# Scan stage of a two-block mixer kernel: first loads ahead of the first gate store, four reload slots, an earlier mask, 14 gate products moved forward

## The chip, the cores and the metric

One core of one Trainium2 chip. The metric is the device time of one execution in microseconds (us). TensorE is called PE here, its weight load PEld, VectorE DVE, ScalarE ACT, GpSimd POOL, and SyncE, which issues the DMAs, SP.

## The reference, cut to what matters

The program computes two blocks. The second one, `hybrid_layer`, projects the normalised input to all its streams, runs four mixers, and adds them with gates:

```python
h = rmsnorm(x, norm_gain)
proj = h @ w_in
(gdn_qkv, gdn_a, gdn_b, gdn_z, sg_u, sg_v, sg_z, rw, rw_z,
 nsa_q, nsa_kv, nsa_g, nsa_z, merge) = jnp.split(proj, IN_OFFSETS, axis=-1)
ys = (gated_deltanet(...), spatial_gating(...), rwkv7_time_mix(...), native_sparse_attention(...))
gates = jnp.split(jax.nn.sigmoid(merge), N_MIXERS, axis=-1)
mixed = gates[0] * (ys[0] @ w_branch[0])
for i in range(1, N_MIXERS):
    mixed = mixed + gates[i] * (ys[i] @ w_branch[i])
return x + mixed @ w_out
```

`merge` is 4096 columns wide (32 tiles of 128) for 1024 positions. It doesn't depend on the mixers, so its product can be done at any time before the end. Spatial gating multiplies by weights that are masked to be causal.

## The kernel before, in words

Activations lie transposed, 128 features on the partitions and 1024 positions in the free dimension. Each float32 product is made of three float32r matmuls (high by high, high by low, low by high), so every operand is kept as a high part and the remainder. Weights come as one stream of chunks of eight 128x128 blocks: SP loads a chunk into one of three raw slots (L294), ACT rounds it to its high part (L304), POOL subtracts for the low part (L312), and PE waits for the low part. The two split chunks are reused as soon as PE has used the chunk two before.

The stages that matter here are these.

**Projections** (`hybrid_in_*`). For each of 30 tiles PE makes 24 matmuls (L359), DVE scales the result into one of four stage buffers (L2558), ACT applies a function (L2606) where the tile has one, and SP stores it to HBM (L2640). Entries 22 to 27 of the list are plain copies, the last two go through Silu. After the last tile DVE multiplies the spatial gating weights by a triangular mask (L2586, 128x512), and then every engine passes a fence ("hy projected"): PE waits for the last instruction of DVE, ACT and POOL. SP waits for these and for the last four stores as well.

**Scans** (`scans_*`). Every engine runs the same order, written as Python generators. `weave_beside` takes turns between two streams: stream 0 is the gated delta net (gdn) and then the first part of the sparse attention (nsa), stream 1 is spatial gating (sg) and then rwkv. Each turn is a weave step. After each step comes one step of a third generator, the gates, and at the steps listed in `MORE_GATES` come more of them. A gate step on PE is one product of the `merge` projection: three 128x512 matmuls at L454. There are 512 of them, two halves of the positions (q) by 32 tiles (m) by 8 input blocks (i). Counting from 0, product 256 q + 8 m + i is the i-th of tile m. Two gate steps after a tile's last product come, on their engines, its scaling in PSUM (DVE L2681), its sigmoid (ACT L2698), its store to HBM (SP L2721), and on SP the load of a further weight chunk. Each engine executes its instructions in this order, so an engine that waits holds back everything behind the waiting instruction.

**The second half of the gates.** The first half (q = 0) uses the split left by the entry, for positions 0 to 511. For q = 1 the same buffers are filled again: in gate steps 250 to 257, one block i each, SP loads x from HBM into a slot of `XB` (L2716), ACT makes the high part (L2703) once product 248 + i has used the old one, DVE the low part (L2685), and product 256 + i waits for that. There are two slots. The loads of blocks 0 and 1 go out with the store of tile 29 (gate step 241); that of block i + 2 waits on SP for the low part of block i.

**Where the order puts them.** There are 381 weave steps on PE, and `MORE_GATES` adds 70, so 451 products lie among the scans. Before weave step s the number of products done is s - 1 plus the extras of the steps below s: 13 before step 2, 250 at the last of step 213, 255 at the last of step 215. SP has 374 steps and takes the same extras.

**Start of the scans on SP.** After the fence SP issues three loads for gdn and its `zy` (L2766), then the 13 gate steps of weave step 1, which hold the store of gate tile 0 (gate step 9) and so wait for it, and then in steps 2 and 4 the six loads of spatial gating, three for each j. PE's first instruction of step 2 is the spatial mean (L2847), which waits for the three of j = 0.

**Attention** (`attend_streams`). 24 gate steps lead, then eight attention streams are woven with the gate steps that are left, one after each step: 512 - 451 - 24 = 37 products, at attention steps 1 to 37 of 233. Attention itself is PE L3999, L4005 and L4011, DVE L4028 to L4042, ACT L4056 and L4062. Then follow the branch products, the output product and the last norm.

Of the kernel before, what the change touches and what calls it, by code (L numbers as in the profile page):

```python
# [835 lines left out]
def wait_steps(n):  # L836
    for _ in range(n):
        yield
# [1598 lines left out]
def mixer1_sync(sy, K, M, chunk0):  # L2437
# [8 lines left out]
               *[("copy", 0)] * 6, *[("silu", 0)] * 2]  # L2446
NP = len(PROJECTIONS)
NM = 32
FUNCTIONS = {"silu": ACT.Silu, "gelu": ACT.Gelu_apprx_tanh, "copy": ACT.Copy, "sigmoid": ACT.Sigmoid}

# [94 lines left out]
def hybrid_in_vector(ve, K, H):  # L2545
    V = K.V
# [16 lines left out]
    def evac(g):  # L2563
# [12 lines left out]
        elif kind == "shift":  # L2576
            ve.own().tensor_tensor(st, pd[:, 2:2 + T], pd[:, 3:], SUB).then_inc(*V())
            ve.own().scalar_tensor_tensor(out=st, in0=st, scalar=K.vec("rw_mu", arg), in1=pd[:, 3:], op0=MUL, op1=ADD).then_inc(*V(("staged", g)))
        elif kind == "copy":
            scaled_into(st, "hp", g, slice(0, 128), ("staged", g))  # L2580
        else:
            scaled_into(st, "hp", g, slice(0, 128), ("plain", g))

    project2_drive(chain((0,), walk(ve, K, nothing, 8, NP, first=1)), evac, small_rows_vector(ve, K, H))
    ve.wait_ge(*K.at("hybrid constants"))
    ve.own().tensor_tensor(H.sg_w[:, :, :], H.sg_w[:, :, :], K.upper.unsqueeze(1).to_broadcast([128, 4, 128]), MUL).then_inc(*V(("causal sg",)))  # L2586
    ve.fence(K, "hy projected")
# [87 lines left out]
def gates_vector(ve, K, N, R):  # L2675
# [7 lines left out]
    def between(i):  # L2683
        ve.wait_ge(*K.at("second high", i))
        ve.own().scalar_tensor_tensor(out=H[:, 1, i, :], in0=R.XB[:, i % 2, :], scalar=N.gain(i), in1=H[:, 0, i, :].bitcast(F32), op0=MUL, op1=SUB).then_inc(*K.V(("second low", i)))  # L2685

# [3 lines left out]
def gates_scalar(se, K, N, R):  # L2690
# [9 lines left out]
    def between(i):  # L2700
        se.wait_ge(*K.at("second x", i))
        se.wait_ge(*K.at("used", i))
        se.own().activation(H[:, 0, i, :], R.XB[:, i % 2, :], ACT.Copy, scale=N.gain(i)).then_inc(*K.S(("second high", i)))  # L2703

# [7 lines left out]
def gates_sync(sy, K, N, R, chunk0):  # L2712
    def second(i):
        if i >= 2:
            sy.wait_ge(*K.at("second low", i - 2))
        sy.e.dma_start(R.XB[:, i % 2, :], K.keep[:, i, HIGH]).then_inc(*K.x_in[i % 2](("second x", i)))  # L2716

    def evac(q, m):
# [4 lines left out]
        if (q, m) == (0, NM - 3):  # L2723
            second(0)
            second(1)

    def between(i):
        if i + 2 < 8:
            second(i + 2)

# [1414 lines left out]
class Scans:  # L4145
    def __init__(self, K, H):
# [3 lines left out]
        self.gates = K.sb([128, 2, 512], ctx=self.late_scope, name="gates")  # L4150
        self.XB = K.sb([128, 2, 512], ctx=self.late_scope, name="xb")
        self.right_scope = Scope("right")
# [16 lines left out]

MORE_GATES = {1: 12, 18: 3, 51: 2, 59: 5, 96: 2, 133: 4, 139: 5, 176: 2, 213: 3, 215: 3, 252: 6, 256: 8, 297: 7, 351: 2, 361: 6}  # L4170

# [40 lines left out]
def in_turn(*streams):  # L4212
    for s in streams:
        yield from s
# [53 lines left out]
def scans_sync(sy, K, R, chunk0):  # L4268
    g, s, w, B = R.gdn, R.sg, R.rw, R.nsa

    def rwkv_first():
        yield from wait_steps(12)
        for j in range(2):
# [6 lines left out]
    weave_beside(gates, in_turn(gdn_sync(sy, K, g, lambda: nsa_load(sy, K, B)), nsa_sync(sy, K, B)),  # L4280
                 in_turn(rounds(spatials(lambda j: spatial_sync(sy, K, s, j)), rwkv_first()), wait_steps(RWKV_LATER), rwkv_sync(sy, K, w)), more=MORE_GATES)

# [674 lines left out]
def program(nc, A, at):  # L4957
    with Scope() as ctx:
# [19 lines left out]
        K.xs, K.w_raw, K.stage_out = ([K.dma(f"{n}{i}") for i in range(k)] for n, k in (("x", 4), ("w", NRAW), ("stage", NSTAGE)))  # L4978
        K.x_in, K.gate_out = ([K.dma(f"{n}{i}") for i in range(2)] for n in ("xh", "go"))
        K.back, K.gate_back = [K.dma(f"y{i}") for i in range(2)], [K.dma(f"g{i}") for i in range(3)]  # L4980
# [40 lines left out]
```

## Time and profile before

| | |
|---|---|
| time, median of 3 runs | 4180.58 us (4179.37 to 4186.12) |
| the profiled execution's own time | 4175.23 us |
| its span, first to last instruction | 4173.4 us |
| mean granted TensorE clock | 0.964 |
| PE busy | 3898.7 us (93%) |
| DVE busy | 2679.8 us (64%) |
| ACT busy | 1449.4 us (35%) |
| POOL busy | 1202.5 us (29%) |
| chain that ended last | PE 71%, DVE 21%, ACT 4% |

All times inside the program count from the start of the span. The scans run from about 2875 to 3750 us, the attention from there to 3958 us. Busy shares are over the span; a wait of PE inside a stage with PE in its chain is what a change can win back. A granted clock of 1.00 is the higher level of PE's clock, 2.4 GHz, and 0.50 the lower one, 1.2 GHz.

### The profile page before, as it was taken

The page shows a single profiled execution, that of the slowest core. Times are in us where ns is not written, and L with a number is a line of the kernel's source. Part 1 is how long each engine was busy: PE and PEld are TensorE (multiplying, and loading weights), DVE is VectorE, ACT ScalarE, POOL GpSimd, SP SyncE. Part 2 cuts the span into 40 slices and gives each one's busy share as a digit, 9 for nine tenths or more (in the row PEclk, how much of TensorE's full clock was granted, in tenths as well). Part 3 has the DMA queues.
Part 4 walks back from the last instruction along what each step waited for, and adds up shares of the span by engine and source line. Part 5 has one row for each costly group of instructions (what it writes and reads, how often), then busy time and mean ns, then how long its engine had stood idle before and what let it go on. Part 6 is the DMA issues. An engine that isn't in the chain of part 4 may idle for free.

```text
span 4173.4 us, 47439 instructions
## 1 busy us (share of the span) xinstructions
PE 3898.7 (93%) x18382; PEld 3094.4 (74%) x18382; DVE 2679.8 (64%) x3001; ACT 1449.4 (35%) x1896; POOL 1202.5 (29%) x583
## 2 busy tenths in 40 slices
PE   8999899999879999989999988998999989998988
PEld 6557788877656666778887867886788878876777
DVE  6764787889764554378778988531655555546783
ACT  4334432234333333243223433212333333325512
POOL 2002134445413333213444531222222112212054
PEclk9999999999989999999999999998999989999999
DMA  3002223345320000222334532223211221323054
GB/s 110 20 16 81 101 91 104 96 153 189 115 76 21 21 26 21 86 101 87 113 104 158 172 119 105 98 101 113 83 62 54 71 76 61 110 73 106 22 206 141
DMA packets 130874, 382.36 MB, mean 92 GB/s; under 512 B 13460, under 2 KB 14104, under 8 KB 125400
## 3 DMA queue, kind: packets, MB, share of 16 engines
q1 hardware_dynamic: 130648, 379.32, 27.4%
q8 instruction: 145, 2.38, 0.2%
q14 instruction: 81, 0.66, 0.1%
HBM read 278.08 MB, written 101.19 MB: 91 GB/s over the span
## 4 chain that ended last, share of the span: by engine, by line
PE 71%; DVE 21%; ACT 4%; issue 1%; DMA 1%; POOL 1%; SPq 0%; DVEq 0%; ACTq 0%; POOLq 0%
PE ps L359 22%; PE ps L1389 20%; PE ps L454 7%; PE ps L872 3%; PE ps L2875 2%; PE ps L2881 2%; PE ps L4342 2%; PE ps L2182 1%; DVE acc L1658 1%; PE ps L2174 1%; DVE top L1562 1%; DVE xop L1562 1%; PE ps L2936 1%; DVE x L636 1%; PE ps L2862 1%
## 5 line engine op out<-in xcount | busy, mean ns | idle before, releaser
L312 POOL TENSOR_TENSOR wlo<-wraw,whi 128x1024 fp32r<-128x1024 f32 x185 | 455.7, 2463 | 1764.8 <-ACT whi L304 1630.9
L1389 PE MATMUL ps<-xop,whi 128*128 128x512 f32 x1984 | 616.7, 392 | 15.5 <-DVE acc L1683 10.1
L304 ACT ACTIVATE whi<-wraw 128x1024 fp32r<-128x1024 f32 x185 | 196.0, 1060 | 907.6 <-PE ps L359 626.4
L1389 PE MATMUL ps<-top,whi 128*128 128x512 f32 x1488 | 470.0, 397 | 22.3 <-DVE acc L1652 17.0
L1389 PEld LDWEIGHTS ps<-xop,whi 128*128 128x128 f32 x1984 | 372.2, 188 | 100.2 <-DVE acc L1683 12.6
L1389 PE MATMUL ps<-xop,wlo 128*128 128x512 f32 x992 | 387.7, 391 | 0.0
L454 PE MATMUL ps<-xhalf,whi 128*128 128x512 f32 x1024 | 363.6, 437 | 4.8 <-ACT n L4056 3.5
L1389 PEld LDWEIGHTS ps<-top,whi 128*128 128x128 f32 x1488 | 281.5, 190 | 91.1 <-DVE acc L1652 20.3
L359 PE MATMUL ps<-xhi,whi 128*128 128x512 f32 x900 | 322.9, 441 | 23.2 <-DVE xlo L656 6.7
L1784 POOL TENSOR_TENSOR wlo<-wsum,whi 128x1024 fp32r<-128x1024 f32 (+2 forms) x102 | 229.4, 2249 | 368.0 <-ACT whi L1414 367.4
L1389 PE MATMUL ps<-top,wlo 128*128 128x512 f32 x744 | 294.5, 396 | 0.0
L359 PE MATMUL ps<-xlo,whi 128*128 128x512 f32 x900 | 286.6, 400 | 0.0
L359 PE MATMUL ps<-xhalf,whi 128*128 128x512 f32 x1012 | 274.9, 394 | 11.2 <-DVE xhalf L656 8.8
L359 PE MATMUL ps<-xhi,wlo 128*128 128x512 f32 x900 | 284.2, 397 | 0.0
L1784 POOL TENSOR_TENSOR wlo<-wraw,whi 128x1024 fp32r<-128x1024 f32 (+2 forms) x80 | 180.1, 2251 | 244.3 <-ACT whi L1414 242.5
L359 PEld LDWEIGHTS ps<-xhi,whi 128*128 128x128 f32 x900 | 169.2, 196 | 86.5 <-issue 34.3
L359 PEld LDWEIGHTS ps<-xhalf,whi 128*128 128x128 f32 x1012 | 191.6, 190 | 53.7 <-DVE xhalf L656 10.7
L1389 PEld LDWEIGHTS ps<-xop,wlo 128*128 128x128 f32 x992 | 186.5, 188 | 41.1
L454 PEld LDWEIGHTS ps<-xhalf,whi 128*128 128x128 f32 x1024 | 173.5, 196 | 46.9 <-issue 21.6
L1414 ACT ACTIVATE whi<-wsum 128x1024 fp32r<-128x1024 f32 (+2 forms) x108 | 101.8, 943 | 304.0 <-PE ps L1389 126.4
L454 PE MATMUL ps<-xhalf,wlo 128*128 128x512 f32 x512 | 205.7, 402 | 0.0
L359 PEld LDWEIGHTS ps<-xlo,whi 128*128 128x128 f32 x900 | 175.2, 195 | 39.1
(625 smaller groups left out, 7424.7 us busy)
## 6 DMA issues: line engine op xcount, KB each, us to landing
wraw<-in_w_dram SPq DMA_DIRECT2D x185, 512.0 KB, 3.7
h_keep<-h SPq DMA_DIRECT2D x154, 256.0 KB, 4.8
wraw<-in_s_dram SPq DMA_DIRECT2D x48, 512.0 KB, 4.2
f<-h_keep SPq DMA_DIRECT2D x24, 768.0 KB, 5.7
wmore<-in_s_dram SPq DMA_DIRECT2D x32, 512.0 KB, 4.2
x_keep<-x SPq DMA_DIRECT2D x16, 1024.0 KB, 3.9
g_keep<-gates SPq DMA_DIRECT2D x64, 256.0 KB, 2.4
gb<-g_keep SPq DMA_DIRECT2D x32, 512.0 KB, 3.6
```

Source lines behind the costliest of these rows:

```text
L304: se.own().activation(K.hi(c), K.raw[:, c % NRAW, :], ACT.Copy).then_inc(*K.S(("hi", c)))
L312: ge.own().tensor_tensor(K.lo(c), K.raw[:, c % NRAW, :], K.hi(c).bitcast(F32), SUB).then_inc(*K.G(("lo", c)))
L359: done = pe.e.matmul(into[:, h, :], wt, x[h], start=(first and j == 0), stop=(last and j == 2), skip_group_check=True)
L454: done = mm(K.ps[:, b, :], wt, x, start=(i == 0 and j == 0), stop=(i == n - 1 and j == 2), skip_group_check=True)
L872: d = mm(K.ps[:, banks[h], :], M.diag[:, (BY_PE.index(j) * TAPS + k) % NDIAG, :], M.Yc[:, j, 512 * h + k:512 * h + k + 512], start=(k == 0 ...
L1389: d = pe.e.matmul(out[:, s, :], w[:, o], x[:, i, :], start=(j < 3 and i == 0 and t == 0), stop=(i == k - 1 and t == 2), skip_group_check=True)
L1414: se.own().activation(F.whi(c), F.source(b, j), ACT.Copy).then_inc(*K.S((n, "whi", c)))
L1562: ve.own().tensor_tensor(F.olo[j][:, :k, :], source[:, :k, :], F.ohi[j][:, :k, :].bitcast(F32), SUB).then_inc(*K.V((F.name, "op", g, j)))
L1784: seat.own().tensor_tensor(F.wlo(c), F.source(b, j), F.whi(c).bitcast(F32), SUB).then_inc(*signal((F.name, "wlo", c)))
L2875: d = mm(K.ps[:, b, part(i)], I.AT[:, part(i)], I.T[:, part(i)], start=True, stop=True, skip_group_check=True)
L2881: d = mm(K.ps[:, b, part(i)], I.X[:, part(i)], I.TT[:, part(i)], start=True, stop=True, skip_group_check=True)
L4342: done = mm(into, w, x, start=(i == 0 and j == 0), stop=(i == 7 and j == 2), skip_group_check=True)
```

## The change

The mask on the spatial gating weights goes from the end of the projections to just after the first plain copy (entry 22). `XB` gets four slots and four semaphores, so the loads of blocks 0 to 3 go out together and that of block i + 4 waits for the low part of block i. `MORE_GATES` gets 14 more products, at or before nine steps. On SP a list of its own, `LOADS_AHEAD`, gives the extras of step 1 at step 4.

```diff
+COPIES = [g for g, (kind, _) in enumerate(PROJECTIONS) if kind == "copy"]
+NXB = 4
 ...
         elif kind == "copy":
             scaled_into(st, "hp", g, slice(0, 128), ("staged", g))
+            if g == COPIES[0]:
+                ve.wait_ge(*K.at("hybrid constants"))
+                ve.own().tensor_tensor(H.sg_w[:, :, :], H.sg_w[:, :, :], K.upper.unsqueeze(1).to_broadcast([128, 4, 128]), MUL).then_inc(*V(("causal sg",)))
 ...
     project2_drive(chain((0,), walk(ve, K, nothing, 8, NP, first=1)), evac, small_rows_vector(ve, K, H))
-    ve.wait_ge(*K.at("hybrid constants"))
-    ve.own().tensor_tensor(H.sg_w[:, :, :], H.sg_w[:, :, :], K.upper.unsqueeze(1).to_broadcast([128, 4, 128]), MUL).then_inc(*V(("causal sg",)))
     ve.fence(K, "hy projected")
 ...
     def second(i):
-        if i >= 2:
-            sy.wait_ge(*K.at("second low", i - 2))
-        sy.e.dma_start(R.XB[:, i % 2, :], K.keep[:, i, HIGH]).then_inc(*K.x_in[i % 2](("second x", i)))
+        if i >= NXB:
+            sy.wait_ge(*K.at("second low", i - NXB))
+        sy.e.dma_start(R.XB[:, i % NXB, :], K.keep[:, i, HIGH]).then_inc(*K.x_in[i % NXB](("second x", i)))
 ...
         if (q, m) == (0, NM - 3):
-            second(0)
-            second(1)
+            for i in range(NXB):
+                second(i)
 
     def between(i):
-        if i + 2 < 8:
-            second(i + 2)
+        if i + NXB < 8:
+            second(i + NXB)
 ...
-        self.XB = K.sb([128, 2, 512], ctx=self.late_scope, name="xb")
+        self.XB = K.sb([128, NXB, 512], ctx=self.late_scope, name="xb")
 ...
-MORE_GATES = {1: 12, 18: 3, 51: 2, 59: 5, 96: 2, 133: 4, 139: 5, 176: 2, 213: 3, 215: 3, 252: 6, 256: 8, 297: 7, 351: 2, 361: 6}
+MORE_GATES = {1: 15, 7: 2, 18: 3, 51: 2, 59: 5, 86: 2, 92: 3, 96: 2, 133: 5, 139: 5, 176: 3, 213: 3, 215: 4, 217: 1, 252: 6, 256: 8, 297: 7, 351: 2, 361: 6}
+LOADS_AHEAD = {**MORE_GATES, 1: 0, 4: 15}
 ...
-                 in_turn(rounds(spatials(lambda j: spatial_sync(sy, K, s, j)), rwkv_first()), wait_steps(RWKV_LATER), rwkv_sync(sy, K, w)), more=MORE_GATES)
+                 in_turn(rounds(spatials(lambda j: spatial_sync(sy, K, s, j)), rwkv_first()), wait_steps(RWKV_LATER), rwkv_sync(sy, K, w)), more=LOADS_AHEAD)
 ...
-        K.x_in, K.gate_out = ([K.dma(f"{n}{i}") for i in range(2)] for n in ("xh", "go"))
+        K.x_in, K.gate_out = ([K.dma(f"{n}{i}") for i in range(k)] for n, k in (("xh", NXB), ("go", 2)))
```

With the 14 more, 465 products lie among the scans and 23 in the attention. Before weave step 213 twelve more are done than before, so products 248 to 255 come at weave steps 202 to 209 and gate steps 250 to 257 at steps 204 to 211, one after each step, where they were at steps 213 to 217.

## Rows read from the trace of the kernel before

**Rows 1.** The page: shares of the chain that ended last, by engine.

```profile
PE 71%; DVE 21%; ACT 4%; issue 1%; DMA 1%; POOL 1%; SPq 0%; DVEq 0%; ACTq 0%; POOLq 0%
```

**Rows 2.** Waits between 2870 and 3766: who for whom, total, times, longest.

```profile
PE ps L2936 <- DVE r L3549: 15.2, 3, 12.2
```

**Rows 3.** Timeline of the scans' start: start, duration, instruction, [idle before it].

```profile
2871.87 2.36 POOL L312 TENSOR_TENSOR wlo<-wraw,whi 128x1024 fp32r<-128x1024 f32 x1 [8.45 <-ACT whi L304]
...
2872.07 2.70 DVE L2586 TENSOR_TENSOR sgw<-sgw,const 128x512 f32<-128x512 f32 x1
...
2874.88 2.08 PE L2847 MATMUL ps<-rows,c 4*128 4x512 f32 x4 [4.23 <-DVE sgw L2586]
...
2876.88 1.22 PE L454 MATMUL ps<-xhalf,whi 128*128 128x512 f32 x2
...
2877.09 0.43 SPq L2766 DMA_DIRECT2D zy<-p_keep  x1
...
2886.10 0.62 PE L454 MATMUL ps<-xhalf,whi 128*128 128x512 f32 x2
...
2886.78 0.62 PE L454 MATMUL ps<-xhalf,whi 128*128 128x512 f32 x2
...
2888.21 3.23 SPq L2766 DMA_DIRECT2D sg<-p_keep  x6
...
2897.08 3.78 PE L2847 MATMUL ps<-sg,c 128*128 128x512 f32 x4 [9.45 <-DMA sg<-p_keep]
...
2901.41 1.84 PE L2781 MATMUL ps<-c,g 128*128 128x2 f32 x16
...
2910.82 3.42 PE L2781 MATMUL ps<-c,sg 128*128 128x2 f32 x16 [1.83 <-ACT sg L2821]
```

**Rows 4.** Stretches at the lower clock: length, PE busy (matmuls), granted clock, DMA.

```profile
2890.55:2900.79 10.24, 3.71 (x5) 0.50 0.80 322
2911.03:2917.86 6.83, 6.83 (x29) 0.50 0.39 115
...
3382.07:3399.14 17.07, 5.79 (x23) 0.50 0.38 123
3402.55:3409.38 6.83, 5.06 (x18) 0.50 0.37 115
...
sum 78.51, PE 57.53; mean PE 4.79
```

**Rows 5.** Timeline around the reload: SP's loads, POOL, PE's waits.

```profile
3375.98 14.18 SPq L2716 DMA_DIRECT2D xb<-x_keep  x6
...
3386.87 2.39 POOL L312 TENSOR_TENSOR wlo<-wraw,whi 128x1024 fp32r<-128x1024 f32 x1 [12.03 <-ACT whi L304]
...
3393.35 2.07 PE L2936 MATMUL ps<-r 64*128 64x128 f32 x8 [12.24 <-DVE r L3549]
...
3404.32 2.08 PE L2936 MATMUL ps<-r 64*128 64x128 f32 x8 [3.75 <-DVE inv L3504]
```

**Rows 6.** High and low parts of the reload: minimum, median, maximum ns, first and last start.

```profile
L2703 ACT ACTIVATE xhalf<-xb,vec x8: 721/722/725, 3374.4 to 3402.0; 128x512 fp32r<-128x512 f32 x8
L2685 DVE SCALAR_TENSOR_TENSOR xhalf<-xb,vec,xhalf x8: 750/751/2169, 3375.2 to 3402.8; 128x512 fp32r<-128x512 f32 x8
```

**Rows 7.** Windows: length, busy PE, PEld, DVE, ACT, POOL, clock, DMA, GB/s.

```profile
3354.50:3368.50 14.00, 14.00 (x103) 12.77 (x102) 10.22 (x21) 9.79 (x15) 6.18 (x3) 1.00 0.23 69
3354.50:3410.40 55.90, 39.90 (x230) 34.62 (x230) 39.11 (x60) 23.18 (x32) 10.99 (x5) 0.79 0.31 99
3795.00:3811.00 16.00, 16.00 (x85) 13.30 (x84) 11.50 (x35) 13.59 (x25) 4.84 (x2) 1.00 0.41 125
3811.00:3958.00 147.00, 129.76 (x790) 98.61 (x788) 113.16 (x381) 89.59 (x217) 7.64 (x4) 0.98 0.04 14
```

**Rows 8.** Two of four smaller waits of PE among the scans: timeline.

```profile
3103.95 1.13 PE L2936 MATMUL ps<-g 64*128 64x128 f32 x8 [2.75 <-DVE g L3089]
...
3197.45 1.84 PE L2936 MATMUL ps<-r 64*128 64x128 f32 x8 [2.62 <-DVE r L3549]
```

More of the change, by code:

```diff
@@ L2684, in between @@
         ve.wait_ge(*K.at("second high", i))
-        ve.own().scalar_tensor_tensor(out=H[:, 1, i, :], in0=R.XB[:, i % 2, :], scalar=N.gain(i), in1=H[:, 0, i, :].bitcast(F32), op0=MUL, op1=SUB).then_inc(*K.V(("second low", i)))
+        ve.own().scalar_tensor_tensor(out=H[:, 1, i, :], in0=R.XB[:, i % NXB, :], scalar=N.gain(i), in1=H[:, 0, i, :].bitcast(F32), op0=MUL, op1=SUB).then_inc(*K.V(("second low", i)))
     yield from gate_tiles(lambda: walk(ve, K, nothing, 8, NM), evac, between)
@@ L2702, in between @@
         se.wait_ge(*K.at("used", i))
-        se.own().activation(H[:, 0, i, :], R.XB[:, i % 2, :], ACT.Copy, scale=N.gain(i)).then_inc(*K.S(("second high", i)))
+        se.own().activation(H[:, 0, i, :], R.XB[:, i % NXB, :], ACT.Copy, scale=N.gain(i)).then_inc(*K.S(("second high", i)))
     yield from gate_tiles(lambda: walk(se, K, weights_scalar, 8, NM), evac, between)
```

## The prediction

> **What bounds the kernel now.** I read the page's chain first: PE holds 71% of it [rows 1], so time is lost where PE waits or runs at its lower clock. The list of waits then names who made it wait among the scans; its longest wait of PE is 12.2 us, for DVE L3549 [rows 2]. The timeline around each long wait gives the places. There are two large ones. At the start PE stands still for 9.45 us until the spatial gating loads land at 2897.08; SP issued them only at 2888.21, behind the store of gate tile 0 [rows 3]. At the reload for the second half PE stands still for 12.24 us and then for 3.75 us [rows 5]. SP spends 14.18 us on its last six loads, because each waits for a slot of two, and DVE, which must make the low parts in order, reaches L3549 late. Four more waits of 2.0 to 2.8 us lie between; two are in [rows 8]. After most of these PE runs at a granted clock of 0.50: the twelve stretches at 0.50 from 2873 to 3461 contain 57.53 us of busy PE [rows 4]. In the attention's gate steps the reader is to see PE full, 16.00 of 16.00 us, and after the last product at 3811 not full, 129.76 of 147 [rows 7].
>
> **The change, part by part.**
>
> *The mask.* It takes 2.70 us of DVE, 2872.07 to 2874.77, and PE starts 0.11 us later, at 2874.88 [rows 3]. Without it the fence still waits for POOL's last low part, 2871.87 + 2.36 = 2874.23. PE then starts at 2874.34: gain 0.54 us, not 2.7. In its new place the 2.70 us lie beside PE's products of the next tile, with DVE idle between tiles; if that cover were gone it would cost 2.7.
>
> *First loads ahead.* SP's loads for gdn and `zy` end at 2877.52 [rows 3] and stay, since they wait for the last projection store. Now only one gate step follows before the loads of sg j = 0, so they go out from about 2877.6 instead of 2888.21. The three landed 2897.08 - 2888.21 = 8.9 us after the first issue. The same delay gives 2886.5; if they also queue behind gdn and `zy`, at most some 3 us more, 2889.5. PE meanwhile has 16 products instead of 13. The 13 took 2876.88 to about 2887.6, 10.75 us; a further one takes 2886.78 - 2886.10 = 0.68 us [rows 3]. So PE reaches the spatial mean at 2876.34 + 10.75 + 2.04 = 2889.1. Against 2897.08 that is 7.9 us, the mask's 0.54 in it; I take 7.6 for the loads' spread. What is late next is neither DMA nor the gate store (tile 0 is ready at about 2887.4, and SP's six loads are out by 2881), but ACT: its split of the chunk behind product 15 now stands at the end of step 1. It has nothing urgent behind it.
>
> *The clock there.* With no idle stretch at 2888 to 2897 the stretch 2890.55 to 2900.79 need not be at 0.50; its 3.71 us of busy PE would take 1.86 [rows 4]. The wait of 1.83 us at 2910.82 [rows 3] gets two products (1.36), and what follows it, 6.83 us busy at 0.50 [rows 4], could give 3.4. The waits behind are chains over POOL and DVE, which don't shrink with the clock. I take 1.8 for the first and nothing to 5.3 for the rest, value 1. Start in all: 7.6 + 1.8 + 1 = 10.4 us, bounds 6 and 15.
>
> *Four slots.* By the weave's count the eight pairs of high and low part come at steps 204 to 211 instead of 213 to 217, one per step. Loads of blocks 0 to 3 go out nine steps ahead, the others four steps ahead of use, with 2 to 3 us per step; the DMA waits vanish. The pairs cost the same work: 8 x 0.75 on DVE, 8 x 0.72 on ACT [rows 6]. Queued behind each low part is all that DVE does for both streams, and PE waits for that. The new place is the window 3354.5 to 3368.5, where PE is full, DVE busy 10.22 and ACT 9.79 of 14 us [rows 7]. With the pairs added they have 16.2 and 15.6 us for 14, so this window stretches by at least 2.2 us. In exchange the wait at L3549 shrinks. For the whole passage, 3354.5 to 3410.4, the floors are: PE 39.90 busy, of which 5.79 + 5.06 at 0.50 [rows 4], so 39.9 - 5.4 + two products more, 35.9 us; DVE 39.11 busy less 1.4 for its one long low part, plus some 0.03 between 60 instructions, 39.5 us. The passage can't fall below 39.5 of 55.9, a gain of 16.4. From the other side, if each pair stalls DVE by one more microsecond and the waits for DVE of 2.62 us remain as in the earlier unit at 3197.45 [rows 8], it is 39.5 + 8 + 2.6 = 50.1, a gain of 5.8. I take 44.5, nearer to the floor, because two steps lie between product 248 + i and its pair: gain 11.4 us.
>
> One long low part stands in [rows 6]: 2169 ns against a median of 751, begun while POOL's L312 of 3386.87 ran [rows 5]. The Trainium skill, "GPSIMD Engine Reference", section "Specifications", says that POOL shares its way into SBUF with DVE and that DVE instructions with two SBUF inputs contend with it. A low part has two. By that rule POOL's 6.18 us of the new window [rows 7] would hit three or so of the eight low parts, at 1.4 us each, and the passage would be 48.7 instead of 44.5; by the trace's other seven low parts, hardly any.
>
> *Fourteen more products.* Three are counted above. Eleven go before waits: two before the 1.83, two before a wait of 2.4, three before 2.75, one each before 2.62 and 2.0, two in the reload passage. There they fill idle time and don't move the end of a wait. If the gap is gone or elsewhere they cost 0.68 each; the seven at the four middle places could lose 4.8. On the other side, shorter idle stretches may keep the clock up: the stretches behind these four places hold about 20 us of busy PE in the sum of [rows 4], 10 us to win. I take 2, near the low end, since the waits shrink and stay.
>
> *The end.* The products leave the attention's steps 24 to 37. There PE is full, 16.00 us for 14 products and the attention's share [rows 7], so 14 x 0.68 = 9.5 us leave the bound. The next bound is DVE, 11.50 busy in that window, 1.4 of it gate scaling, and its density afterwards is 113.16 / 147 = 77% [rows 7]: 10.1 / 0.77 = 13.1, a gain of 2.9. ACT loses its gate work as well (13.59 busy falls most). The 24 leading products stay 24, and attention's first loads go out as before. Bounds 2.9 and 9.5; I take 7, because the whole stretch from 3776 has less PE and ACT work, not only this window.
>
> *Sum.* 10.4 + 11.4 + 2 + 7 = 30.8 us. The profiled execution took 4175.23 us (span 4173.4 and 1.8 around it), 5.35 under the median of the runs, 4180.58. So 4144.4 for it, and 4149.8, say 4150, as a median.
>
> **The rivals.**
> 1. *The reload's stall only moves.* DVE and ACT are over-full in steps 204 to 211, and in order, so PE waits there instead. For it: 16.2 us of DVE work for 14. Against: DVE and ACT have 17 and 33 us free in the whole passage. The passage gains 5.8, the middle -2 and the end 2.9: 10.4 + 5.8 - 2 + 2.9 = 17, time 4163.
> 2. *The clock stays up.* The twelve stretches hold 57.53 us of busy PE, 29 to win. For it: waits of 9.45 and 12.24 us stand just before the two longest. Against: stretches follow waits of 2.0 us too. With the start at 15, the passage at 16, the middle at 6 and the end at 9: 46, time 4135. The Trainium skill, "TensorE: Matmul & The Clock Gate", section "Part 1: The HAM clock gate", has it that the throttled state is the default and activity lifts it; by that rule products in place of waits pay twice, as here. The trace agrees as to the order of events [rows 4].
> 3. *Slower.* The low part waits for the high part of the same gate step, and the high part for product 248 + i; where DVE, ACT and PE take turns on these waits, the eight steps become a chain, and everything of both streams waits in it. It costs eight times the price of a turn. The stalls that it replaces are 12.24 + 3.75 = 16 us and the other parts give 19.4, so it decides the sign from 35.4 / 8 = 4.4 us a step. With 6 us a step: 48 - 35.4 = 13 slower, 4193. Against: PE needs low part i only six products later.
> 4. *The loads don't come earlier*, because the change's order on SP meets a wait that I don't see. Then only three filled products and the fence remain at the start, 1 us instead of 10.4: 4159.
>
> **How the numbers follow.** Forecast 0.60, rival 1 0.18, rival 2 0.12, rival 4 0.06, rival 3 0.04. The forecast's own terms reach 22 to 40 us of gain, 4141 to 4159. With rival 1 whole and most of rival 2, the range is 4136 to 4168. The measurement tells changes of 0.2%, 8.4 us, from none. Faster than that: forecast, rivals 2 and 4, and 0.14 of rival 1: 0.92. Within 0.2%: 0.05. Slower: 0.03.
>
> **What would show it.** PE's mean L2847 starts near 2889 with no wait for DMA above 1 us. PE's first L2847 waits for POOL's L312 rather than for DVE. SP's eight loads of `xb` don't spread over 24 us but the first four go out in 2 us, and ACT L2703 waits for no DMA. The wait for L3549 falls from 12.2 to under 4 us, and the window of the eight pairs is 2 to 5 us longer. The last L454 product comes some 30 us before 3811. It would be wrong if the passage takes over 50 us, or if attention from its first product to its end keeps its length.

## The result and the profile after

| | median us | range | runs |
|---|---|---|---|
| before | 4177.85 | 4167.89 to 4186.47 | 20 |
| after | 4187.49 | 4179.94 to 4193.81 | 20 |

The ratio is 1.0022, 95% interval 1.0015 to 1.0029: the change makes the kernel 9.6 us slower, where 4150 was forecast, with 0.03 for slower.

The profiled execution of the changed kernel took 4185.32 us, its span is 4183.5, PE is busy for 3909.2 us (before 3898.7) at a mean clock of 0.965, DVE 2684.5, ACT 1452.8, POOL 1208.0. From line 2587 of the kernel before up to its list `MORE_GATES` a line's number is 3 higher in the changed kernel (L2681 is L2684, L2698 is L2701, L2847 is L2850, L2936 is L2939, L3549 is L3552). The page's chain, which answers to [rows 1]:

```profile
PE 69%; DVE 23%; ACT 4%; issue 1%; POOL 1%; DMA 1%; DVEq 0%; SPq 0%; ACTq 0%; POOLq 0%
```

The waits of PE between 2870 and 3766, which answer to [rows 2] (total us, times, longest):

```profile
PE ps L2865 <- ACT g L2841: 9.3, 3, 4.4
PE ps L2939 <- DVE r L3552: 5.0, 3, 2.4
PE ps L2850 <- DVE r L3542: 4.0, 2, 3.2
PE ps L2850 <- POOL wlo L312: 3.8, 1, 3.8
```

The wait of 12.2 us is gone. At the top stands a new one: PE waits for L2841, a copy out of PSUM on ACT.

The start, timeline (as [rows 3]):

```profile
2878.40 1.13 PE L2850 MATMUL ps<-rows,c 4*128 4x512 f32 x4 [3.84 <-POOL wlo L312]
...
2881.47 3.24 SPq L2769 DMA_DIRECT2D sg<-p_keep  x6
...
2892.09 1.88 PE L2850 MATMUL ps<-sg,c 128*128 128x512 f32 x4
```

The loads go out before any gate store, the mean waits for nothing and begins 13.7 us after PE's first scan instruction; before it was 2897.08 - 2874.88 = 22.2 us [rows 3].

The reload, timeline and the durations of low and high parts (as [rows 5, 6]):

```profile
3347.49 1.89 SPq L2719 DMA_DIRECT2D xb<-x_keep  x4
...
3366.26 6.15 SPq L2719 DMA_DIRECT2D xb<-x_keep  x4
...
3387.30 1.10 PE L2850 MATMUL ps<-r,c 128*128 128x512 f32 x2 [3.20 <-DVE r L3542]
```

```profile
L2706 ACT ACTIVATE xhalf<-xb,vec x8: 723/726/727, 3363.8 to 3382.1; 128x512 fp32r<-128x512 f32 x8
L2688 DVE SCALAR_TENSOR_TENSOR xhalf<-xb,vec,xhalf x8: 750/752/1721, 3365.5 to 3382.9; 128x512 fp32r<-128x512 f32 x8
```

The passage and the attention behind its last product, windows (as [rows 7]); in a window of 56 us around the reload PE now gets through 322 matmuls and is busy for 50.5 us, where it was 230 and 39.9 of 55.9:

```profile
3358.00:3414.00 56.00, 50.54 (x322) 42.83 (x320) 42.74 (x67) 30.51 (x43) 13.42 (x6) 0.97 0.30 95
3814.00:3962.00 148.00, 128.65 (x755) 95.82 (x755) 115.17 (x394) 88.88 (x221) 7.06 (x3) 0.98 0.04 13
```

Lastly the whole stretch from PE's first scan instruction to the first matmul of the projection behind the attention, with PE alone (window, length, busy PE, its matmuls, clock, DMA), and behind it the sum over those parts of it in which the granted clock is 0.50. First the kernel before:

```profile
2874.90:3959.00 1084.10, 1009.90 (x6243) 0.96 0.23 73
...
sum 97.59, PE 76.21; mean PE 4.76
```

The changed kernel:

```profile
2878.40:3969.20 1090.80, 1020.84 (x6243) 0.95 0.23 73
...
sum 98.96, PE 92.80; mean PE 5.46
```

The reader is to see three numbers. Idle PE: 74.2 us before, 70.0 after, so the products did fill idle time. Busy PE at the lower clock: 76.2 before, 92.8 after. Matmuls take about twice as long there (a pair of L454 1.22 us at 0.50 and 0.62 at 1.00 [rows 3]), so half of the 16.6 more is lost, 8.3 us. The rest, busy time less half of the low part, is 971.8 and 974.4. Together -4.2 + 8.3 + 2.6 = +6.7 us, the growth of the stretch; the other 3.5 of the span lie ahead of it. There the profiles differ by more than that from one execution to the next: PE's first scan instruction starts at 2878.4 in this one and at 2868.5 in that of e8 below, whose projections are the same. So from here on I compare times that count from this instruction.

To see where, I compare the start of each PE instruction in both traces, relative to the first scan instruction. Minus is earlier than before:

| at (time before) | after against before | what lies in between |
|---|---|---|
| 2923 | -14.4 us | start without the wait for loads |
| 2962 | -2.3 | new waits of 1.80 and 4.38 us, and 17 us at the lower clock |
| 3350 | +4.2 | small waits, some filled, some new |
| 3418 | -7.2 | reload: 11.4 us won |
| 3527 | +1.6 | new wait of 3.54 us and 13.7 us at the lower clock |
| 3663 | +10 | |
| 3766 | +15.8 | |
| 3958 | +6.8 | attention, with 14 products fewer, 9.0 us won |

Start, reload and end give what was forecast for them or more. Between them 12.1 + 6.5 + 8.8 + 14.2 = 41.6 us are lost, at places where the forecast had a gain of 2. The products themselves are the small part of it. Five of the fourteen lie in the start and two in the reload; the other seven all lie between 2962 and 3350, 7 x 0.68 = 4.8 us if each costs its full price. The remaining 12.1 + 8.8 + 14.2 = 35.1 us are lost in stretches to which no product was added.

**The loss at 2937 to 2955.** Timeline of the changed kernel:

```profile
2932.49 2.45 POOL L312 TENSOR_TENSOR wlo<-wraw,whi 128x1024 fp32r<-128x1024 f32 x1 [9.04 <-ACT whi L304]
2933.49 2.00 DVE L2894 TENSOR_TENSOR inv<-inv,c 128x512 f32<-128x512 f32 x1
...
2936.37 0.63 PE L2865 MATMUL ps<-const,inv 128*128 128x128 f32 x4 [1.80 <-DVE inv L2895]
...
2937.97 1.22 DVE L3333 TENSOR_TENSOR sg<-sg 128x1024 f32<-128x1024 f32 x1
2939.30 0.70 DVE L2684 TENSOR_TENSOR ps<-ps,t 128x512 f32<-128x512 f32 x1
2940.03 0.60 ACT L2701 ACTIVATE gates<-ps 128x512 f32<-128x512 f32 x1 [6.35 <-DVE ps L2684]
...
2940.72 1.29 ACT L2841 ACTIVATE g<-ps 128x512 f32<-128x512 f32 x2
...
2941.37 1.11 PE L2865 MATMUL ps<-const,inv 128*128 128x128 f32 x4 [4.38 <-ACT g L2841]
```

Read it from the end. PE waits for ACT's copy L2841. It is short and its input is there, but ACT is in order, and in front of it stands the sigmoid of a gate tile, L2701. That waits 6.35 us for the tile's scaling L2684 on DVE, and the scaling stands in turn behind spatial gating's and gdn's vector work. So work that PE needs now queues behind work that nobody needs yet. The clock falls 1 us into that wait, at 2937.9, and stays down for 13.6 us behind its end, in which PE is full:

```profile
2937.90:2954.97 17.07, 13.60 (x48) 0.50 0.43 139
```

At 3505 the same chain recurs, again with L2684, L2701, L2841 in a row:

```profile
3502.61 2.43 POOL L312 TENSOR_TENSOR wlo<-wraw,whi 128x1024 fp32r<-128x1024 f32 x1 [6.82 <-ACT whi L304]
3502.79 2.81 DVE L2895 TENSOR_TENSOR inv<-const,inv 128x512 f32<-128x512 f32 x1
...
3507.21 0.70 DVE L2684 TENSOR_TENSOR ps<-ps,t 128x512 f32<-128x512 f32 x1
3507.94 0.60 ACT L2701 ACTIVATE gates<-ps 128x512 f32<-128x512 f32 x1 [5.41 <-DVE ps L2684]
...
3509.23 1.12 PE L2865 MATMUL ps<-const,inv 128*128 128x128 f32 x4 [3.54 <-ACT g L2841]
```

In both places a DVE instruction of gdn's inverse runs beside POOL's split of a chunk and takes 2.00 and 2.81 us where the one next to it takes 0.69. The Trainium skill ("GPSIMD Engine Reference", section "Specifications") has it that POOL contends with DVE instructions that read two SBUF inputs; these do, and the trace agrees. The delay is handed on: DVE is not idle between L2894 and the tile's scaling, so the 1.3 us extra of the first place are part of PE's waits there, and the 2.1 us extra of the second are part of the 3.54.

Both the tile work and the splits hang on the number of products done: a tile is 8 products and its scaling, sigmoid, store and next load come two gate steps behind the eighth. In the kernel before they stand at places where they harm little. The added products shift them: by 3 from step 1 on, by 5 from step 7, 7 from 86, 10 from 92, then 11, 12, 13 and 14. So two theories were put against each other. **Phase**: what costs is the shift of all later tiles against the streams, and a shift by a multiple of 8 costs nothing. **Rivals**: the three scheduling edits are at fault, the products cost their own time, or the count alone matters. In the expectations below theory A is the phase; B has it that the streams' own chains give back what is won; C that a product costs only where it was added.

### The profile page after: what moved, and what is told of

It is laid out like the page before. It is cut to its first block, busy times and chain, and to the rows that moved or that the text cites. A ratio compares the mean times of both kernels' runs of the same rounds, so it can differ in the third digit from the quotient of the medians.

```text
span 4183.5 us, 47429 instructions
## 1 busy us (share of the span) xinstructions
PE 3909.2 (93%) x18382; PEld 3097.0 (74%) x18382; DVE 2684.5 (64%) x3001; ACT 1452.8 (35%) x1896; POOL 1208.0 (29%) x583
## 4 chain that ended last, share of the span: by engine, by line
PE 69%; DVE 23%; ACT 4%; issue 1%; POOL 1%; DMA 1%; DVEq 0%; SPq 0%; ACTq 0%; POOLq 0%
PE ps L359 21%; PE ps L1389 19%; PE ps L454 7%; PE ps L872 3%; PE ps L2878 2%; PE ps L2884 2%; PE ps L4346 2%; PE ps L2182 1%; DVE top L1562 1%; DVE acc L1658 1%; DVE xop L1562 1%; PE ps L2174 1%; PE ps L2939 1%; DVE t L618 1%; DVE x L636 1%
## 5 line engine op out<-in xcount | busy, mean ns | idle before, releaser
L454 PE MATMUL ps<-xhalf,whi 128*128 128x512 f32 x1024 | 363.2, 437 | 8.8 <-POOL wlo L312 5.4
L454 PEld LDWEIGHTS ps<-xhalf,whi 128*128 128x128 f32 x1024 | 174.2, 197 | 51.6 <-issue 24.0
L454 PE MATMUL ps<-xhalf,wlo 128*128 128x512 f32 x512 | 207.8, 406 | 0.0
```

The costliest lines, as they stand in the source:

```text
L454: done = mm(K.ps[:, b, :], wt, x, start=(i == 0 and j == 0), stop=(i == n - 1 and j == 2), skip_group_check=True)
```

## The experiments

The edits below are against the changed kernel or the one named. Each was timed in five rounds beside the kernel before (4177, 4176 for the last two).

| run | median us | range | ratio to before, 95% |
|---|---|---|---|
| e1 three edits, old products | 4162.45 | 4155.1 to 4165.6 | 0.9968 [0.9956, 0.9980] |
| e2 new products only | 4198.95 | 4191.7 to 4208.0 | 1.0059 [1.0047, 1.0071] |
| e3 loads ahead only | 4163.26 | 4155.7 to 4165.0 | 0.9971 [0.9960, 0.9983] |
| e4 four slots only | 4175.88 | 4166.2 to 4182.8 | 0.9994 [0.9984, 1.0004] |
| e5 e1 + 3 products at step 1 | 4185.75 | 4177.1 to 4194.7 | 1.0019 [1.0008, 1.0030] |
| e6 e1 + 8 | 4162.19 | 4160.1 to 4171.7 | 0.9965 [0.9953, 0.9978] |
| e7 e1 + 3, 3 fewer at step 18 | 4165.52 | 4163.6 to 4166.6 | 0.9970 [0.9961, 0.9980] |
| e8 after, tile work 5 steps later | 4186.67 | 4179.0 to 4194.2 | 1.0023 [1.0013, 1.0032] |
| e9b e1 with six slots | 4163.82 | 4161.1 to 4170.3 | 0.9963 [0.9951, 0.9975] |
| e10b e1 + 4 | 4176.96 | 4163.7 to 4187.7 | 0.9997 [0.9987, 1.0007] |
| e11b e1, middle products moved | 4159.22 | 4155.1 to 4167.4 | 0.9952 [0.9940, 0.9963] |
| e12b e5, tile work 3 steps later | 4173.59 | 4167.8 to 4186.8 | 0.9989 [0.9980, 0.9999] |
| f1 e6 and e11b together | 4163.32 | 4150.7 to 4168.0 | 0.9966 [0.9954, 0.9977] |
| f2 after, 8 more products in place of 14 | 4167.49 | 4163.5 to 4171.9 | 0.9979 [0.9970, 0.9988] |

**Which part of the change.** e1 keeps mask, loads and slots and puts the old products back:

```diff
-MORE_GATES = {1: 15, 7: 2, 18: 3, 51: 2, 59: 5, 86: 2, 92: 3, 96: 2, 133: 5, 139: 5, 176: 3, 213: 3, 215: 4, 217: 1, 252: 6, ...}
+MORE_GATES = {1: 12, 18: 3, 51: 2, 59: 5, 96: 2, 133: 4, 139: 5, 176: 2, 213: 3, 215: 3, 252: 6, ...}
```

> Mask, first loads ahead and four slots together, with the 70 extra gate products where they were. Theory A (the 14 added products change which weave step each gate tile is finished at, and the new meeting points cost more than the rest wins): 15 to 25 us faster than before, with the start and the reload each 8 us or more earlier and nothing given back in between. Theory B (the scans are paced by the chains of the streams over DVE, ACT and POOL, which give back what the start and the reload win): within 5 us of before. The time from the first inverse products at 2953 to 3375 is the same as before within 3 us under A, 8 or more longer under B.

e2 is the kernel before with the new list, on SP too.

> Only the 14 more products, on SP as well; mask, loads and slots as before. Theory A: 15 to 30 us slower than before, with new waits of PE of 3 us or more that end on ACT or DVE work for a gate tile, and lower-clock stretches in which PE is full behind them. Theory B: within 5 us of before, since the products fill waits (minus) and the chains keep their pace.

e1 is 0.32% faster than before, 14 us between the medians, and e2 0.59% slower, 22 us between the medians for 14 products; together 1.0027, near the 1.0022 of the whole change. The edits add up, and the products alone make it slower. e1 stays just short of the 15 us of theory A, and nothing is given back from 2953 to 3375 (12.2 us ahead of the kernel before at both ends), which is against B. e2 shows more than the time. It has none of the three scheduling edits, and yet the new waits of the changed kernel stand in it again, to a few hundredths: 1.79 and 4.37 us for 1.80 and 4.38, then 3.19 for 3.20 and 3.54 for 3.54.

```profile
2952.81 1.12 PE L2862 MATMUL ps<-const,inv 128*128 128x128 f32 x4 [4.37 <-ACT g L2838]
```

e3 and e4 part e1 further: e3 has only `LOADS_AHEAD = {**MORE_GATES, 1: 0, 4: 12}` beside the kernel before, e4 only `NXB = 4`.

> Only the first loads ahead of the first gate store (12 extras of step 1 at step 4 on SP). Theory A: 7 to 11 us faster; PE's wait of 9.45 us before the spatial mean falls to under 2 us and the lead is kept to the end. Theory B: the lead is there at 2930 and gone by 2960; within 3 us of before.

> Only the four slots. The high and low parts stay at weave steps 213 to 217. Theory A: the waits for the DMA (8.4 us on ACT) go, PE's wait at L3549 falls from 12.2 to about 5 us, 6 to 10 us faster. Theory B: the same wait falls but the next chain gives it back, within 3 us of before.

The loads alone give 13 of e1's 14 us, more than the 7 to 11 expected: the lead is 12.8 us at 2937 and still 12.3 at 3958. The slots give nothing in the time that can be told from none. In e4's trace PE's wait falls from 12.2 to 9.2 us, not to 5, and the passage from 3350 to 3418 wins 2.6 us; in e1 it wins 4.0, in e3, without slots, 0.9. So the slots are worth some 3 us there. The mask had no run of its own; e3 and e4 leave nothing of e1 for it. Why four slots help so little without the products is in DVE's order in e1:

```profile
3358.61 1.87 SPq L2719 DMA_DIRECT2D xb<-x_keep  x4
3369.20 9.58 SPq L2719 DMA_DIRECT2D xb<-x_keep  x4
...
3374.63 5.52 DVE L2688 SCALAR_TENSOR_TENSOR xhalf<-xb,vec,xhalf 128x512 fp32r<-128x512 f32 x4
3380.18 0.69 DVE L3614 TENSOR_TENSOR r<-r 128x512 f32<-128x512 f32 x1
...
3382.94 0.69 DVE L3552 TENSOR_TENSOR r<-ps,r 128x512 f32<-128x512 f32 x1
...
3383.68 2.07 PE L2939 MATMUL ps<-r 64*128 64x128 f32 x8 [9.36 <-DVE r L3552]
```

With the old products four low parts stand in one block in front of L3552; one of them, beside POOL's split, takes 2.95 us. In the changed kernel the pairs are spread over weave steps 204 to 211, one step each, the last low part starts at 3382.9, and the longest wait for L3552 is 2.4 us. The gain of the reload belongs to the products that moved the pairs, and hardly to the slots: e2, with two slots, wins nearly all of it, going from 15.3 us behind the kernel before at 3350 to 5.0 at 3418. Six slots in place of four (`NXB = 6`) put the question to the transfers once more:

> The kernel e1 (the three scheduling edits, without the added products) with six reload slots in place of four. In e1 the rwkv step at L3552 behind the reload still waits 9.4 us, the transfers of blocks 4 to 7 being issued only as slots come free. DMA reading (the transfer is what is late): with six slots two more blocks are under way early, that wait falls to about 6 us, and the time is 4157 to 4160. In-order reading (VectorE and ScalarE stand in line, the transfer is only reported as last): the wait falls by less than 2 us and the time stays at 4160 to 4164.

The wait falls from 9.36 to 8.31 us and the time stays (4163.82): the in-order reading holds. ACT waits for no load of `xb` at all now, where it was 6.3 us in e1. Even the 1.05 us aren't the transfers': the block of four low parts takes 4.46 us for 5.52, because its longest one, beside POOL's split, takes 1.90 for 2.95.

```profile
3378.73 2.08 PE L2939 MATMUL ps<-r 64*128 64x128 f32 x8 [8.31 <-DVE r L3552]
```

**Phase or count.** To e1, products at the first place only: `1: 15` (e5), `1: 20` (e6), `1: 15, 18: 0` (e7), `1: 16` (e10b), with the number in `LOADS_AHEAD` alike.

> The three edits, and only the first of the added groups: 3 more products in weave step 1 (15 for 12), so that every later product is one of a tile three products ahead of where it was. Theory A (what counts is the phase of tiles and chunks against the weave steps): the lead of the three edits at 2930 is kept or grows by the lower-clock stretch there, and then falls by 5 to 20 us at places where no product was added; in all 3 to 15 us slower than the three edits alone (they took 4162). Theory C (each added product costs only where it was added): the same time as the three edits within 4 us, since three products cost 2 us at the start and give 2 us back at the end.

> The three edits and 8 more products in weave step 1 (20 for 12), a whole tile and chunk, so that phases are as before from step 2 on. Theory A: no new waits between 2900 and 3370; the 5.4 us that the eight products take at the start come back at the end, and the reload falls into other weave steps, where it may win up to 10 us; 4150 to 4162. Theory C: 4158 to 4166. If the number of products done ahead counted rather than their phase, it would be slower than e5.

> The three edits, 3 more products in weave step 1 and 3 fewer at step 18, so that the phases are as before from step 18 on and differ only from step 1 to 18. Theory A: nothing is lost after about 2935 in comparison with before; 4158 to 4168. Theory C: the same. If it loses as e5 does, the loss comes from the first 18 steps and not from the phase later.

> The three scheduling edits, and four more gate products at the first place (16 where e1 has 12, e5 has 15, e6 has 20): every later gate tile's scaling, sigmoid and store, and every chunk's split, move by half a tile. Phase reading (what counts is at which step of the streams a tile's work falls): any time from 4167 to 4190, the time not lying on the line between e1, e5 and e6. Rival, a smooth effect of the number of products: 3 cost 23 us, 8 cost nothing, so 4 lie on the falling side, at about 4181. Rival, e5's three are an unlucky single collision: 4160 to 4165.

Three more cost 23 us, beyond the 3 to 15 that theory A gave; four cost 15, eight nothing. Three more that are taken back at step 18 cost 3, which the intervals don't tell from none. In the traces, relative to e1, PE's instructions in e7 stand at +3.2 us at 3022 and between +1.6 and +3.8 from there to the end, while those of e5 drift to +36.5 (its profiled execution, 4194.69, was its slowest). e6 stands between +3.0 and +6.5 up to 3347, about the 8 x 0.68 = 5.4 us of its own products, and at +6.7 from 3436 to 3726. So the loss of e5 isn't the number of products, nor their own 0.68 us: it is where later tiles and splits fall. That four cost less than three, and eight nothing, a line through the count can't give. The smooth rival's 4181 for four lies just outside the interval, 4171.8 to 4180.2, and the single collision's 4160 to 4165 well outside; the phase's own range of 4167 to 4190 was so wide that it proves little by itself. Whether the cost within a period of 8 is smooth or the sum of several collisions stays open.

A rival within the phase is that the shift only makes more DVE instructions run beside POOL's splits. It doesn't: what all DVE instructions of the scans took beyond the usual time of their line and shape sums, by my estimate from the traces, to 31 us before, 35 in the changed kernel and 30 in e5. What changes is which of them are hit and who waits behind.

e5 shows in full what the lower clock takes. PE waits 1.93 us at 3715.31 for DVE, and then 1.42 us at 3721.30 for a bank that the sigmoid of a gate tile frees late. No further wait above 0.9 us follows before this stretch, with PE full throughout, of which 10 us are lost:

```profile
3735.90:3756.38 20.48, 20.48 (x72) 0.50 0.15 45
```

**Tile work or splits.** e12b is e5 with the tile work three gate steps later, at about its steps in e1, while products and splits stay three early. With a tile's scaling and sigmoid its store and the load of a further chunk move too. e8 does it to the changed kernel, five steps later (`[None] * 6`).

```diff
-                late += [None, (q, m)]
+                late += [None] * 4 + [(q, m)]
```

> The kernel e5 (three scheduling edits, three more products at the first place, 4185.75 us) with a gate tile's scaling, sigmoid and store queued three gate steps later, so that they stand again at about the steps that they have in e1; the chunks' splits and the products themselves stay three early. If the place of a tile's scaling and sigmoid in the orders of VectorE and ScalarE is the cause of e5's 23 us: 4160 to 4170. If it is the splits or the products themselves: 4180 to 4190. Between these, both have a part.

> The changed kernel with one edit: a tile's scaling, sigmoid and store come seven gate steps after its last product instead of two. Products stay where they are, and so do the splits of the chunks. Theory A with the tile's work as the cause: at 2937 the products are five ahead of before, so the tile's work is back at its old weave steps; the wait of 4.4 us for ACT at 2937 and those near 3010 go, and 8 to 15 us are won by 3050; later, where products are 11 to 14 ahead, it wins or loses. Theory A with the chunks' splits as the cause: the waits near 2937 and 3010 stay.

e12b wins back 12 of the 23 us between e5 and e1, between the two ranges: the place of the tile work has about half of it, the splits and the products themselves the rest; I didn't part these two. e8's time is that of the changed kernel, but its course isn't. In it the waits of 1.80 and 4.38 us near 2937 are gone, as the explanation has it, with one of 2.68 in their place, and it is 9.5 us ahead of the changed kernel at 3043, within the 8 to 15 expected, and 15.6 at 3683. From 3707 on it loses all of this, since PE waits before products instead, 4.64, 2.55, 2.94 and 7.41 us, the last for a chunk:

```profile
3777.16 0.70 DVE L2684 TENSOR_TENSOR ps<-ps,t 128x512 f32<-128x512 f32 x1
3777.30 1.06 ACT L304 ACTIVATE whi<-wraw 128x1024 fp32r<-128x1024 f32 x1 [12.07 <-DMA wraw<-in_w_dram]
...
3781.09 1.19 PE L454 MATMUL ps<-xhalf,whi 128*128 128x512 f32 x2 [7.41 <-POOL wlo L312]
```

SP issues the load of a further chunk behind a tile's store. A later store is a later load, and the chunk's split then holds up PE. So the delay isn't free in itself.

**Does it hold for the change as it is?** f2 is the changed kernel with its products up to step 96, then brought back to 8 more:

```diff
-133: 5, 139: 5, 176: 3, 213: 3, 215: 4, 217: 1,
+133: 2, 139: 5, 176: 2, 213: 3, 215: 3,
```

> The changed kernel (4187.49 us) with eight more products than before in place of fourteen: all of its added ones up to step 96, but 2 at step 133 in place of 5, 2 at 176, 3 at 215 and none at 217, so that behind step 139 every tile is back at the step that it had before. The changed kernel lies 12 us behind e1 at that place and 25 at the end. Phase reading: what it loses behind the place goes, what it loses ahead of it stays, 4170 to 4178. Rival (the loss is that of the products themselves, 22 us for 14, evenly): six fewer give back 9 us, 4178 to 4181. Rival (the order behind is no better with the old places once the start has moved): 4184 to 4190.

It takes 4167.49, ratio 0.9979. From the changed kernel's 1.0022 to e1's 0.9968 are 0.54%, 23 us; six products fewer give back 0.43% of it, 18 us, where they themselves are 6 x 0.68 = 4. That is more than either reading had in its range, and twice what the even loss by count has. In the traces, relative to e1, f2 stands at +12.4 us from 3200 to 3345 and at most 3.5 further back from 3430 to 3800, where the changed kernel goes from +9.1 to +32.6. The sum over its lower-clock parts, where the changed kernel has 92.80:

```profile
sum 83.62, PE 73.76; mean PE 5.27
```

Its 17 us stretch at 2936 is still there, ahead of the place where the phase is restored.

**A faster version.** e11b moves products of the middle earlier and leaves their sum as it was: `86: 2, 92: 3, 133: 1` for `96: 2, 133: 4`. f1 has eight more at step 1 beside that.

> The three scheduling edits, and the middle products moved earlier by a few steps with their number unchanged (2 at step 86 and 3 at 92 in place of the 2 at 96 and 3 of the 4 at 133): the waits of 2.4 and 2.8 us of the kernel before at these steps are filled, and behind step 133 every tile keeps its place. Phase reading: between steps 86 and 133 tiles move by 2 to 5 products, which costs or gains a few us, and nothing moves behind: 4157 to 4168, with the waits of 2.4 and 2.8 us under 1.5. Reading by the count alone (a filled wait is won, nothing else matters): 4158 or less.

> The three scheduling edits, eight more gate products at the first place (20 where e1 has 12), and the middle products moved earlier as in e11b. Phase reading: eight keep every tile at its place, so the two changes add up: e6's 4162 and e11b's 4159 give 4156 to 4163. Count reading (products cost about 0.68 us each wherever they fall, and 8 are far from nothing): 4164 to 4170.

e11b is the fastest that I ran, 0.48% under the kernel before; its interval overlaps with e1's, so that the moved products add something isn't shown. In its trace the waits of 2.41 and 2.75 us are 1.03 and 1.84, the second not under 1.5 as expected, and the later one of 2.62 has grown to 4.09. f1 is no better than either, between the ranges of phase and count: it doesn't tell the two apart.

## Why the prediction was wrong

*The mask*, 0.54 us: PE's first wait fell from 4.23 [rows 3] to 3.84, 0.39 us, and is for POOL, as forecast. Right.

*First loads ahead and the clock there*, 10.4: 14.4 us by the traces of the whole change, with the five products that were put in there, and 13 by e3's median without any. Right, at the upper bound. The spatial mean came 8.5 us earlier, for about 7.4 by the forecast's own places; the rest, 5.9, is what followed it, where 2.8 were taken. The stretch at 0.50 at 2890 [rows 4] went with the wait.

*Four slots*, 11.4: the passage did win 11.4 us (+4.2 to -7.2) and the wait for L3552 is 2.4 us, under the 4 that were given as the mark. The size was right, to the tenth by luck with bounds of 5.8 and 16.4, and the owner wrong. I counted the pairs' new weave steps and the slots as one edit; e4, e1 and e9b show that the slots alone win some 3 us there, since DVE's block of low parts, not the transfer, was last, and e2 that the products alone win 10.3. Of the eight low parts one ran beside POOL's split, 1.72 us for 0.75, not three.

*The end*, 7: 9.0 us, right within its bounds.

*Fourteen more products*, 2 us won: this step failed. "There they fill idle time and don't move the end of a wait. If the gap is gone or elsewhere they cost 0.68 each" priced a product by itself, on PE alone. The gaps did fill: 2.41, 2.75, 2.62 us became 1.38, 1.06, 2.39, and PE is idle for 4.2 us less in all. But each product also moves every later tile's scaling, sigmoid, store and load, and every chunk's split, in the orders of DVE, ACT, SP and POOL. I had that shift in hand and used it only where it helped, at the reload ("by the weave's count the eight pairs ... come at steps 204 to 211"). What is theirs in the forecast (the reload's 11.4, the middle's 2, the end's 7) is a gain of 20.4; e2 measured a loss of 22.3, 42.7 us off. The remaining 10.4 were measured as 14.2 in e1. 14.2 - 22.3 = -8.1, against -9.6 for the whole change. What the runs show in place of the missing term: 35.1 us lost where no product was added, 8.3 us more taken by the lower clock over the whole stretch, and 18 us won back by f2 with the old phase behind step 139. How the loss parts between the tile work and the splits stays open.

The forecast's rule for the clock was one-sided too. Rival 2 asked what filled waits give back in granted clock. None asked what short new waits cost: new waits of 1.8 and 4.4 us bring 17 us at 0.50, so that a stall of 6 us costs 12. Rival 3, the one on the slower side, looked for a chain inside the eight pairs; its price of 4193 is near, and its mechanism didn't happen. The two signs that were to show the forecast wrong, a passage over 50 us and an attention of the old length, didn't come either: neither watched the stretches from 2923 to 3350 and from 3418 to 3766, where the time went. One mark did fail, the last L454 product 30 us before 3811: it starts at 3812.4, where it was 3808.9. The base was a little off as well: 4180.58 is the median of three runs, that of twenty is 2.7 us lower, and the same gain would give 4147.

## What to carry to other kernels

Where a filler stream is interleaved with others by an order written out by hand, adding work at one place shifts everything of it that comes later, on every in-order engine. Price the shift, not the piece: list where the filler's side work (evictions, stores, loads, splits) will stand, and see whose waits it will stand in front of. Add or move pieces in multiples of the side work's period, or take them back soon after, and the rest of the schedule stays as it was tuned; here that held for eight products (e6), for three taken back at step 18 (e7) and for f2 behind step 139.

Ask of an edit that frees a buffer whether the transfer or the order of the consuming engine is last; a wait put down to a VectorE instruction says to read what stands in front of it.

## What the runs showed of the hardware

The lower clock can begin and last with next to no idle time of PE. In e5 it falls 13 us behind a wait of 1.42 us, with PE busy for 13.3 of the 14 us from 3722 to 3736, and PE is then full for 20.48 us at 0.50. In the changed kernel it falls 1 us into the wait of 4.38 us at 2937 and stays while PE is busy for 13.60 of 17.07. That the clock was low is seen in the matmuls too: in e5's stretch the pairs of L454 take 1.05 to 1.22 us, in the 14 us ahead of it mostly 0.62 to 0.73. The Trainium skill, "TensorE: Matmul & The Clock Gate", section "Part 1: The HAM clock gate", has activity lift the throttle; here it was busy and not lifted for that long, so the measurement decides. Whether a wait brings the clock down in such a place, or small matmuls do, is open: in e5 sixteen of 64x64 (L3872) and eight of 128x2 (L2784) stand just in front of the fall, and three more groups of sixteen inside the stretch. Why it stays down is left open.

A DVE instruction that reads two SBUF inputs waits out a split that POOL has begun. In the scans of the changed kernel 13 such instructions (tensor_tensor, 128x512, both inputs in SBUF, 0.69 us when alone) start while a split runs, and every one of them ends 0.55 us behind the split's end, whenever it began: they take 0.73 to 2.89 us. Five that started 0.28 us or more ahead of a split took 0.69. Those with an input in PSUM aren't touched: 49 that overlap a split by 0.5 us or more all took 0.70 at the most. The low part of 2.95 us for 0.75 (e1), started 0.05 us ahead of a split, also ends 0.55 us behind it. So does the mask of the kernel before. It starts 0.20 us behind a split and ends with the same delay, so most of its 2.70 us [rows 3] were waiting for POOL. In its new place it again falls beside a split and takes 2.80.
